# Head-pair attention in a one-core decoder layer: the sum of scores and decay kept in PSUM, and the next query tile's scores and maxima issued ahead of the present transposes

## The reference, cut to what matters

```
s = einsum('bqhd,bkhd->bhqk', q, k) * HEAD_DIM**-0.5
s = s + dq[..., None] - dk[:, None, :]      # d = running sum of log forget gates
s = where(k_pos <= q_pos, s, -inf)
p = softmax(s)
att = einsum('bhqk,bkhd->bqhd', p, v)
```

## Time and profile before

| | us |
|---|---|
| median of three runs (2131.2 to 2139.19) | 2134.02 |
| the profiled execution's own time | 2138.08 |
| span of the profiled execution, first to last instruction | 2136.4 |
| TensorE (PE) busy | 2025.6 (95%) |
| VectorE (DVE) busy | 798.0 (37%) |
| ScalarE (ACT) busy | 390.2 (18%) |
| GpSimd (POOL) busy | 632.9 (30%) |
| mean granted TensorE clock | 0.983 |

### The profile page before, as it was taken

The page is one execution under the profiler, slowest core; times in us unless marked ns, Lnnn a source line. Parts: engine busy times, 40 slices in busy tenths (PEclk is TensorE's granted clock), DMA queues, the critical chain, the costliest instruction groups (busy, mean ns, idle before and its releaser), DMA issues.

```text
span 2136.4 us, 33015 instructions
## 1 busy us (share of the span) xinstructions
PE 2025.6 (95%) x13046; PEld 1926.8 (90%) x13046; DVE 798.0 (37%) x1427; ACT 390.2 (18%) x699; POOL 632.9 (30%) x489
## 2 busy tenths in 40 slices
PE   5989988699999999999999998999999999999996
PEld 4978887555899999999999997999999999999996
DVE  3445556544100224012721667144224423341337
ACT  3434444422100000000210244100000000000003
POOL 4321111023432222223232623432322223232323
PEclk9999998999999999999999999999999999999998
DMA  9322112287422112241111401111111111111112
GB/s 329 102 65 61 39 33 81 93 265 254 149 79 79 50 40 90 70 128 40 39 49 49 155 9 30 50 40 49 39 49 39 49 39 45 43 40 48 40 40 84
DMA packets 174968, 164.17 MB, mean 77 GB/s; under 512 B 14254, under 2 KB 138626, under 8 KB 174747
## 3 DMA queue, kind: packets, MB, share of 16 engines
q1 hardware_dynamic: 153451, 132.50, 20.3%
q0 software_dynamic: 6400, 17.05, 2.5%
q10 hardware_dynamic: 15032, 13.43, 2.0%
HBM read 149.03 MB, written 14.03 MB: 76 GB/s over the span
## 4 chain that ended last, share of the span: by engine, by line
PE 84%; DVE 5%; SPq 4%; ACT 2%; issue 2%; DMA 1%; POOL 0%; ACTq 0%; POOLq 0%; DVEq 0%
PE psA L1767 11%; PE psA L1773 11%; PE psA L1771 11%; PE psB L1773 10%; PE psB L1771 10%; PE psB L1767 10%; PE psB L1881 2%; PE psB L1885 1%; PE psB L1884 1%; PE psA L1935 1%; PE psB L2045 1%; DVE prob L1279 1%; PE ps L1949 1%; PE psA L2020 1%; SPq L405 1%
## 5 line engine op out<-in xcount | busy, mean ns | idle before, releaser
L639 POOL CAST whi<-raw 128x1024 fp32r<-128x1024 f32 x131 | 136.7, 1043 | 1143.2 <-PE psA L1767 547.7
L640 POOL TENSOR_TENSOR wlo<-raw,whi 128x1024 fp32r<-128x1024 f32 x131 | 321.7, 2456 | 10.5
L1767 PE MATMUL psA<-hhi,whi 128*128 128x364 f32 x1008 | 223.3, 330 | 3.0 <-DVE stat L1363 1.6
L1773 PE MATMUL psA<-hhi,wlo 128*128 128x364 f32 x1008 | 223.4, 330 | 0.0
L1771 PE MATMUL psA<-hlo,whi 128*128 128x364 f32 x1008 | 223.1, 329 | 0.0
L1773 PE MATMUL psB<-hhi,wlo 128*128 128x364 f32 x960 | 212.5, 330 | 0.0
L1767 PE MATMUL psB<-hhi,whi 128*128 128x364 f32 x960 | 211.9, 329 | 0.6 <-DVE alo L1388 0.6
L1771 PE MATMUL psB<-hlo,whi 128*128 128x364 f32 x960 | 212.5, 329 | 0.0
L1642 DVE TENSOR_TENSOR ft<-psB,sil 128x1092 f32<-128x1092 f32 x22 | 28.5, 1296 | 405.4 <-PE psB L1773 398.2
L1767 PEld LDWEIGHTS psA<-hhi,whi 128*128 128x128 f32 x1008 | 174.8, 189 | 3.8 <-issue 3.4
L1773 PEld LDWEIGHTS psA<-hhi,wlo 128*128 128x128 f32 x1008 | 175.8, 189 | 0.0
(11 more groups left out here) (419 smaller groups left out, 3639.6 us busy)
## 6 DMA issues: line engine op xcount, KB each, us to landing
raw<-in_w_in SPq DMA_DIRECT2D x53, 512.0 KB, 3.9
raw<-in_w_gate_up SPq DMA_DIRECT2D x44, 512.0 KB, 3.8
kpage<-in_cache_k SPq DMA_DIRECT2D x64, 256.0 KB, 4.4
vpage<-in_cache_v POOLq DMA_DIRECT2D x64, 256.0 KB, 4.0
ada_late<-in_ada_w SPq DMA_DIRECT2D x8, 2048.0 KB, 8.1
raw<-in_w_down SPq DMA_DIRECT2D x22, 512.0 KB, 3.8
ada<-in_ada_w SPq DMA_DIRECT2D x4, 2048.0 KB, 18.0
x_keep<-xt SPq DMA_DIRECT2D x1, 4368.0 KB, 21.6
```

The source lines that it names most:

```text
L639: link(nc.gpsimd.tensor_copy(whi[slot][:, 0:n, :], raw[slot][:, 0:n, :]))
L640: nc.gpsimd.tensor_tensor(wlo[slot][:, 0:n, :], raw[slot][:, 0:n, :], whi[slot][:, 0:n, :].bitcast(F32), ALU.subtract).then_inc(s["w_split ...
L1767: m = mm(ps[:, c, 0:CH], whi[slot][:, b, :], hi[:, k, c * CH:(c + 1) * CH], start=first, stop=False)
L1773: m = mm(ps[:, c, 0:CH], wlo[slot][:, b, :], hi[:, k, c * CH:(c + 1) * CH], start=False, stop=last)
```

## The change

Three loops and four waits are changed.

- scores_max writes the sum with the decay back to PSUM, over the scores (psA or psB), and no longer to prob. So it no longer waits for the transposes of tile n - 2.
- exp reads the sum from PSUM and writes prob. It takes over the wait for the transposes of tile n - 2.
- scores of the next pair now wait on `p_done` (the exponentials have read PSUM) where they waited on `mx_done`.
- TensorE's order becomes scores(i + 1), transposes(2i), fill, transposes(2i + 1), fill, fill, values(i).
- VectorE's order becomes scores_max(2i + 2), scores_max(2i + 3), pt_low(2i), fill, pt_low(2i + 1), fill, normalise(2i + 2), normalise(2i + 3), fill.
- ScalarE's order becomes pt_hi(2i), exp(2i + 2), fill, pt_hi(2i + 1), exp(2i + 3), fill, fill, o_copy(i), and the decay rows are loaded one tile earlier, after tile 12.

```diff
@@ def exp(p, n):
                 act.wait_ge(s["mx_done"], p * NTILE + (n + 1))
-                nc.scalar.activation(prob[n % 2][:, 0:w], prob[n % 2][:, 0:w], ACT.Exp, bias=negmax[:, n % 2:n % 2 + 1],
+                if n >= 2:
+                    act.wait_ge(s["tr_done"], p * NG + (LAST_GROUP[n - 2] + 1))
+                elif p:
+                    act.wait_ge(s["tr_done"], (p - 1) * NG + (LAST_GROUP[NTILE - 2 + n] + 1))
+                nc.scalar.activation(prob[n % 2][:, 0:w], flat(GP[n % 2])[:, 0:w], ACT.Exp, bias=negmax[:, n % 2:n % 2 + 1],
@@ ScalarE's loop
                     pt_hi(p, n)
+                    if n + 2 < NTILE:
+                        exp(p, n + 2)
+                    elif p + 1 < HP:
+                        exp(p + 1, n + 2 - NTILE)
                     next(fill, None)
-                    for r in range(2 if n % 2 else 0):
-                        if n + 1 < NTILE:
-                            exp(p, n + 1 + r)
-                        elif p + 1 < HP:
-                            exp(p + 1, r)
                     if n % 2:
                         next(fill, None)
-                    if n == NTILE - 3 and p + 1 < HP:
+                    if n == NTILE - 4 and p + 1 < HP:
                         decay_load(p + 1, 0)
                         decay_load(p + 1, 1)
@@ def scores_max(p, n):
                 dve.wait_ge(s["s_done"], p * NTILE + (n + 1))
-                if n >= 2:
-                    dve.wait_ge(s["tr_done"], p * NG + (LAST_GROUP[n - 2] + 1))
-                elif p:
-                    dve.wait_ge(s["tr_done"], (p - 1) * NG + (LAST_GROUP[NTILE - 2 + n] + 1))
-                link(V.tensor_tensor_reduce(prob[n % 2][:, 0:w], flat(GP[n % 2])[:, 0:w], decay[:, r, 0:w],
+                sums = flat(GP[r])[:, 0:w]
+                link(V.tensor_tensor_reduce(sums, sums, decay[:, r, 0:w],
                                             1.0, NEG, ALU.add, ALU.max, rowmax[:, n % 2:n % 2 + 1]))
@@ VectorE's loop
-                for n in range(NTILE):
-                    pt_low(p, n)
-                    next(fill, None)
-                    if n % 2 == 0:
-                        continue
-                    ahead = (p, n + 1) if n + 1 < NTILE else (p + 1, 0)
+                for n in range(0, NTILE, 2):
+                    ahead = (p, n + 2) if n + 2 < NTILE else (p + 1, 0)
                     for r in range(2 if ahead[0] < HP else 0):
                         scores_max(ahead[0], ahead[1] + r)
+                    for r in range(2):
+                        pt_low(p, n + r)
+                        next(fill, None)
                     for r in range(2 if ahead[0] < HP else 0):
                         normalise(ahead[0], ahead[1] + r)
                     next(fill, None)
@@ def scores(p, i):
                     if p:
-                        pe.wait_ge(s["mx_done"], p * NTILE)
+                        pe.wait_ge(s["p_done"], p * NTILE)
...
-                    pe.wait_ge(s["mx_done"], p * NTILE + 2 * i)
+                    pe.wait_ge(s["p_done"], p * NTILE + 2 * i)
@@ TensorE's loop
                 for n in range(NTILE):
+                    if n % 2 == 0 and n + 2 < NTILE:
+                        scores(p, n // 2 + 1)
+                    elif n % 2 == 0 and p + 1 < HP:
+                        scores(p + 1, 0)
                     transposes(p, n)
                     next(fill, None)
-                    if n % 2 and n + 1 < NTILE:
-                        scores(p, n // 2 + 1)
-                    elif n % 2 and p + 1 < HP:
-                        scores(p + 1, 0)
                     if n % 2:
                         next(fill, None)
                         values(p, n // 2)
```

## The result

The changed kernel took 2163.14 us (median of four runs, 2160.69 to 2164.93) against 2133.64 before (four runs, 2131.2 to 2139.19): ratio 1.0138, 95% interval 1.0123 to 1.0153, **29.5 us slower**. Its profiled execution's own time is 2163.11, its span 2161.5 and the mean granted clock 0.976, against 2138.08, 2136.4 and 0.983.

A forecast was written before the change was run, and what follows sets the result against it. TensorE, busy for 95% of the span, was taken as the bound, so the change wins only where it idles. 15.6 (filled head pairs) + 5.7 (last) - 0.8 = +20.5 us on 2134.0 gave 2154.5 us, range 2123 to 2171.

The forecast's parts named there:

- Waits on normalise go: TensorE's waits on normalise, 10.6 us in all, vanish except at the very start, where 0.8 us is credited once.
- The last head pair, +5.7: Last head pair, without fill: transposes and values wait longer behind maxima and exponentials, 3.3 + 2.4 = +5.7 us.
- The filled head pairs, 11.6 us each: Head pairs filled with the next one's projections: waits 11.6 us against 6.3, +5.2 each, +15.6 us for three.
- The third group: Filled head pairs, pairs 4 and 7: third fill group waits for a copy behind pt_hi and exponential, 2.1 and 1.7 us.
- Idle time together: Whole kernel: the sum of all terms, 15.6 + 5.7 - 0.8 = +20.5 us.
- PSUM, 0: Maximum written to PSUM and exponential reading it there: taken as 0 us more.
- Clock, 0: TensorE's granted clock: more idle argues for more low clock, one stretch costing 1.7 us, but 0 was taken.
- the waits on normalise were the whole matter: Rival: VectorE and ScalarE have room, so pt_low and bank copies come no later; about 2120 us, chance 0.17.
- only the last head pair pays: Rival: fill covers its own bank copies in the filled head pairs; no change, 2140 us, chance 0.20.
- the bank takes turns: Rival: reading and writing one PSUM bank doubles the maximum's column time; 2181 us, chance 0.08.

The follow-up runs named there:

- e2: Kernel before with the sum kept in PSUM and the new loops in the last head pair only; 2143.05 us, ratio 1.005.
- e1: Changed kernel's PSUM edit alone, with the three loop orders of the kernel before; 2132.82 us, ratio 1.0001.
- e5: Changed kernel with pt_low(2i) between the two maxima on VectorE instead of behind both; 2145.07 us, ratio 1.0066 against the kernel before.
- e3: Kernel before with the sum kept in PSUM and the new loops in the filled head pairs only; 2149.57 us, ratio 1.0082.
- e4: Changed kernel with ScalarE's copies of the fill's bank ahead of the exponential; 2163.45 us, ratio 1.0154 against the kernel before.
- e6: Changed kernel with fill pieces spread, one between scores and transposes, and the old order in the last head pair; 2134.41 us, ratio 0.9999 against before.
- e7: Changed kernel with 8 unread matmuls behind transposes(2i) in pairs 1 to 7 of the last head pair; 2157.23 us, ratio 1.0119 against before.
- e8: Kernel before with unread matmuls in the last head pair, 4 behind transposes(2i) and 3 behind values; 2131.22 us, ratio 0.9995.
- e9: Kernel before with VectorE's split of k cut in two and unread matmuls in the last head pair; 2127.16 us, ratio 0.9974.

## Why the prediction was right and wrong

Forecast 2154.5 us (2123 to 2171), measured 2163.1. The direction, the queue mechanism and the places were right; the size fell 9 us short. It would have fallen shorter still if the count of idle time had not been 3.6 us too high: two errors offset each other in part, and that is luck.

- **Waits on normalise go.** Right: none is left. The first idle spell, 3.07 us before the first transposes, has become 2.19 us before scores(1), which wait for the exponential: 0.9 shorter (0.8 credited).
- **The last head pair, +5.7.** Measured +7.1 of idle time, +7.6 in e2 against e1, so this was too low. 1.3 of it is the wait for GpSimd's split of v, which the prediction took as unchanged. In pair 6 transposes(13) start 3.70 after transposes(12), the 3.7 foretold, and values 2.12 later, as foretold.
- **The filled head pairs, 11.6 us each.** Measured 9.8. Pair by pair, foretold and measured: pair 0 1.2 and 1.13, pair 1 0.9 and 0.91, pair 2 0.6 and 0.61, pair 4 2.1 + 2.1 and 1.99 + 1.58, pair 5 0.8 + 0.65 and 0.59 + 0.63, pair 6 0.9 and 0.75, pair 7 0.7 + 1.7 and 0.62 + 1.07. The third group was put too late twice, by 0.5 and 0.6: there the count of ScalarE's queue was too long. Three times 9.8 - 6.3 is +10.5, not +15.6 (+9.7 with the 0.9 of the first spell in it).
- **Idle time together.** Foretold +20.5, measured +16.9 (table). This part was too large.
- **PSUM, 0.** Right: e1, 1.0001. By the overheads of the Trainium skill ("Perfetto Trace Analysis", section "Optimizing Scalar/DVE Operations") each maximum could be 0.065 us longer, an estimate from its figures. The trace agrees in part: the maximum itself isn't longer, its accumulator read is 141 ns instead of 83, but the two maxima start 1.40 us apart (417.88 to 419.28) against 1.39.
- **Clock, 0. This is the step that failed.** It measured +10.2 us of slower matmuls in the stretch (+11.1 by the page): 4.4 in the last head pair, 5.7 in the filled ones, where the prediction had no lower clock at all. The prediction saw that more idle time argues for more of the low level, priced one stretch at 1.7 (at its granted 0.59 the 3.5 us cost 1.4), and then took 0 because the rows of before showed no simple rule. The rule is still not simple, but zero was the one value that the argument spoke against. Against e1, busy time rises by 1.5 us with 7.6 of idle time in e2, 3.3 with 7.2 in e5, 3.7 with 10.9 in e3, 8.5 with 18.5 in e4 and 10.4 with 16.7 in after: more idle time, more of it, but not in proportion. The busy share alone doesn't size it either. The last head pair has 0.80 at 66% busy in e2 and 0.73 at 68% in after, and the filled ones lost clock while TensorE was still busy for 88% of the time.
- **The rivals.** That the waits on normalise were the whole matter: fell, by after and again by e6, where even a harmless form of the order wins nothing. That only the last head pair pays: fell, e3 +17.1. That the bank takes turns: fell, e1.

What stays open is what exactly sets the clock. Between 370.7 and 389 us of after TensorE was busy 14.86 of 18.3 us and had 0.53; in the 2 us behind, almost idle, the records say 1.00. No experiment here isolates the pattern. The Trainium skill ("TensorE: Matmul & The Clock Gate", section "HAM oscillation — how this bites in real kernels") describes a kernel whose matmul bursts are parted by DMA waits, so that each burst starts at the lower clock. The traces agree in direction (0.74 in after's last head pair, 0.95 in e7's), but those DMA waits are longer than the waits here: after's last head pair has none above 2.75 us, and the filled ones lose clock behind waits of 1.99 and 1.58.

## What to carry to other kernels

Work issued ahead is free only for the engine that issues it: on each in-order queue it passes, ask what short evacuation now stands behind it, and who waits for that one (e5: moving one maximum gave back over half; e4: easing one queue lengthened another). Cost a new wait on TensorE at more than its length: here 17 us of idle time came with 10 us of slower matmuls, and not only in the partly filled head pair. And before reordering the whole loop, look at the longest single wait: cutting one 2 us block in front of pt_low in two was worth more (-5.8 us, interval some -2 to -7) than any form of the large change.

## What the runs showed of the hardware

- A maximum written in place to the PSUM bank that it reads isn't slower (1232 and 1222 ns against 1225 at 1024 columns), but its accumulator read shows 141 ns in place of 83 (142 in e1). It isn't felt: two maxima in a row start 1.40 us apart, against 1.39 before.
- The exponential gains less than 40 ns by reading PSUM, 1116 ns against 1154, and its accumulator read takes back some (195 and 208 ns against 186).
- Matmuls that no one reads made the changed kernel faster by some 4 to 6 us (e7). For the faster ones (e8, e9) no gain can be told, though the clock rose in all three.
- In the filled head pairs of after, waits of 1.99 and 1.58 us at pair 4 were followed by 6.8 us at half clock, at the same place in each of the two that ran at full clock before.
- Over 72 executions of the kernel before on four chips, 0.001 of granted clock goes with some 1.5 us in 2130.
